# Gate products and pool channels by one level of Strassen's scheme, with reordered weight sums on GpSimd

## Chip, cores and metric

The kernel runs on one core of a Trainium2 chip. The metric is device time in microseconds (us), from runs of the whole program on that core. The engines are TensorE (PE, with its weight loads shown apart as PEld), VectorE (DVE), ScalarE (ACT), GpSimd (POOL) and SyncE (SP), which only issues transfers here.

## What is computed

One decoder layer over 512 tokens of width 1024, in fp32. The part that matters here is the head of it:

```
h = rmsnorm(x, g_mix[i])
u = h @ w_in[i]                       # 1024 -> pool 512 | q 512 | k 128 | v 128
y_a = pool_mixer(u_pool, w_pool_mix[i], pool_scale[i]) @ w_branch_a[i]
y_b = swa_attention(q, k, v, q_gain[i], k_gain[i], attn_sinks[i]) @ w_branch_b[i]
gates = jax.nn.sigmoid(h @ w_gate[i] + b_gate[i])      # 1024 -> 2048
merged = gates[..., :D] * y_a + gates[..., D:] * y_b
x = x + merged @ w_out[i]
```

`pool_mixer` takes, for each of four groups of 128 channels, the trailing mean over 2, 4, 8 or 16 tokens minus the token, and mixes the channels. The attention has 8 heads of 64 and a window of 128, and is done in four blocks of 128 tokens. Behind this stand a routed layer of 64 experts (three matrices of 1 MB each for every expert, 192 MB in all), a shared expert, and a last gated addition.

## The kernel before

The activations h are kept transposed in `actT` (128 partitions x 8 k-blocks x 512 tokens). Weights arrive in `ring`, 12 slots of 1 MB. The list `DENSE` gives the order of the weight units of the head: q0, q1, kv, pool0, pool1, gate0 to gate7, wa0, wb0, wa1, wb1, out0 to out3, shg, shu; `DENSE_SLOT` gives their slots. SyncE loads them in this order (`load_dense`, L419), each after the unit that had its slot before has been used (`released_by`, L416). Every engine runs its instructions in the order in which its block of the program is written; semaphores with names such as `pool_ps` or `gate_copied` connect them.

PE works in this order:
- the q, k, v products for four tiles of 128 tokens (L1500: 512 columns, L1506: 256 columns, 8 k-blocks each), with the transposes of q and k (L1519, L1521) behind the next tile. DVE normalises each tile in between (L982 to L998) and copies the transposes out (L974, L976), with POOL making the reciprocal roots (L621, L622);
- the pool channels: four tiles of 128 channels, 8 matmuls of 128x128 weights against 512 tokens each, into banks 0 to 3 (L1540). ACT copies them out (L758), POOL makes the windowed means (L645 to L651);
- the scores of block 0 (L1571), then 16 gate tiles (`gate_tile`, L1556), 8 matmuls of 512 columns each, alternating between PSUM banks 0 and 1. ACT copies each out with its bias (L772), and tile m waits until tile m-2 has been copied. In between stand four attention rounds: transposes of the probabilities (`probs_T`, L1588), scores of the next block, a gate tile, attention times values (`attend`, L1600), a gate tile. Four gate tiles, the pool mixing (`mix`, L1609) and two more gate tiles end it;
- the branch products wa and wb (L1641, L1643), then w_out (L1659) and what follows.

DVE does softmax: scores plus bias (L1023), maximum (L1028), small operations (L1029 to L1031), the division (L1036 to L1038), and it copies the transposed probabilities (L1048) and the attention output (L1052). ACT takes the exponentials (L764). After the last gate tile ACT makes the sigmoids of all gates (L789), and DVE multiplies and adds (L1068 to L1073).

In the expert stage PE does for each step 64 records of gate and up products (L1904) and 32 of the down product (L1933). SyncE loads an expert into its slots after PE has used what is there (L450, L469).

## Time and profile before

| | us |
|---|---|
| median of 3 runs | 1023.71 (1023.64 to 1026.5) |
| the profiled execution | 1023.04 |
| its span, first to last instruction | 1020.8 |
| PE busy | 952.3 |
| DVE busy | 297.5 |
| ACT busy | 166.2 |
| POOL busy | 167.7 |

Median and profiled execution differ by 0.67 us; 2.2 us lie around the span. Busy time of PE counts matmul records, whose ends overlap, so durations of one record are longer than the pace at which they follow each other; the chain of what ended last gives the pace. A matmul in fp32 shows as two records, each with its own weight load.

### The profile page before, as it was taken

To read this page: it belongs to the slowest core of one execution; us is meant where nothing else is said; L and a number is where in the kernel's file an instruction comes from. 1 tells how busy PE (TensorE), PEld (TensorE's weight loads), DVE (VectorE), ACT (ScalarE), POOL (GpSimd) and SP (SyncE) were. 2 spreads that over 40 slices of the span, in tenths; PEclk is the share of its full clock that TensorE was granted. 3 is DMA by queue.
4 is the path that set the end of the run, shared out by engine and by line. 5 is a ranking of instruction groups with operands and counts; after the bars stand their busy time and mean duration, and the time that the engine had idled before them with its cause. 6 is when DMAs were issued, how large, how long until landed. Compare 5 with 4: busy or idle time off the path is not lost.

```text
span 1020.8 us, 14891 instructions
## 1 busy us (share of the span) xinstructions
PE 952.3 (93%) x6015; PEld 418.7 (41%) x6015; DVE 297.5 (29%) x707; ACT 166.2 (16%) x308; POOL 167.7 (16%) x319
## 2 busy tenths in 40 slices
PE   6999999999999999999999999989969998984698
PEld 4554544444445543443333333345323333331244
DVE  3322552002224743333332111111101111110677
ACT  2002221122001121111111111111111112111021
POOL 4236000000000012222222222212121212111010
PEclk9999999999999999999999999999989999998799
DMA  9441211210191589999999999999999999996982
GB/s 336 138 146 61 83 42 42 82 67 17 40 344 42 204 316 347 417 409 412 405 412 405 411 418 401 394 416 414 397 422 421 421 421 421 418 403 256 376 298 83
DMA packets 82148, 294.90 MB, mean 289 GB/s; under 512 B 9148, under 2 KB 35680, under 8 KB 57888
## 3 DMA queue, kind: packets, MB, share of 16 engines
q1 hardware_dynamic: 67472, 255.90, 63.8%
q0 software_dynamic: 11920, 33.86, 8.5%
q10 hardware_dynamic: 2688, 4.19, 1.1%
q8 instruction: 48, 0.79, 0.3%
q14 instruction: 20, 0.16, 0.1%
HBM read 277.14 MB, written 25.17 MB: 296 GB/s over the span
## 4 chain that ended last, share of the span: by engine, by line
PE 72%; DMA 23%; DVE 2%; SPq 1%; issue 1%; ACT 0%; POOL 0%; POOLq 0%; DVEq 0%; ACTq 0%
PE ps L1904 21%; DMA ring<-in_w_exp_up 19%; PE ps L1556 11%; PE ps L1933 7%; PE ps L1659 5%; PE ps L2030 4%; PE ps L1540 3%; PE ps L1500 3%; PE ps L1643 3%; PE ps L1641 3%; PE ps L1477 2%; DMA ring<-accumulator 2%; DMA ring<-in_w_exp_down 1%; PE ps L1730 1%; PE ps L1506 1%; SPq L450 1%
## 5 line engine op out<-in xcount | busy, mean ns | idle before, releaser
L1904 PE MATMUL ps<-ring,gates 128*32 128x512 f32 x2560 | 288.5, 603 | 28.4 <-DMA ring<-in_w_exp_up 27.7
L1904 PEld LDWEIGHTS ps<-ring,gates 128*32 128x32 f32 x2560 | 88.1, 111 | 220.9 <-issue 220.0
L1933 PE MATMUL ps<-ring,poolbuf 128*32 128x512 f32 x1280 | 145.6, 595 | 3.0 <-DMA ring<-in_w_exp_down 3.0
L1318 DVE COPY poolbuf<-ps 128x256 f32<-128x256 f32 x40 | 17.0, 425 | 357.6 <-PE ps L1913 357.6
L1556 PE MATMUL ps<-actT,ring 128*128 128x512 f32 x256 | 112.3, 595 | 0.0
L661 POOL TENSOR_TENSOR tickets<-cst 128x1 f32<-128x1 f32 x77 | 14.6, 189 | 398.2 <-ACT actT L850 392.7
L1556 PEld LDWEIGHTS ps<-actT,ring 128*128 128x128 f32 x256 | 47.9, 190 | 59.6 <-issue 59.5
L1933 PEld LDWEIGHTS ps<-ring,poolbuf 128*32 128x32 f32 x1280 | 37.9, 109 | 83.4 <-issue 81.7
L850 ACT ACTIVATE actT<-ps,qT 128x1024 f32<-128x1024 f32 x40 | 44.6, 1114 | 142.2 <-PE ps L1933 142.2
L842 ACT ACTIVATE poolbuf<-ps 128x256 f32<-128x256 f32 x40 | 15.4, 385 | 281.6 <-PE ps L1904 281.6
L2030 PE MATMUL ps<-ring,actT 128*128 128x512 f32 (+1 forms) x144 | 59.8, 568 | 0.5 <-DVE actT L1434 0.5
L1477 PE MATMUL ps<-cst,rows 128*128 128x128 f32 x352 | 48.1, 283 | 9.4 <-DMA cst<-in_constants 9.1
L1659 PE MATMUL ps<-ring,gates 128*128 128x512 f32 x128 | 56.4, 594 | 0.0
L621 POOL TENSOR_SCALAR st<-st 128x1 f32<-128x1 f32 (+2 forms) x17 | 5.0, 295 | 289.2 <-ACT rows L795 227.8
L1477 PEld LDWEIGHTS ps<-cst,rows 128*128 128x128 f32 x352 | 44.5, 193 | 11.0 <-DMA cst<-in_constants 9.1
L673 POOL DMA_INDIRECT rows<-h_rows,stage x40 | 41.9, 1048 | 21.7 <-issue 19.3
L678 POOL DMA_INDIRECT accumulator<-actT,stage x40 | 40.7, 1019 | 21.8 <-issue 21.8
L2030 PEld LDWEIGHTS ps<-ring,actT 128*128 128x128 f32 x144 | 27.8, 199 | 25.4 <-issue 23.8
L1659 PEld LDWEIGHTS ps<-ring,gates 128*128 128x128 f32 x128 | 23.8, 190 | 27.3 <-issue 27.3
L1068 DVE TENSOR_TENSOR gates<-gates,ps 128x512 f32<-128x512 f32 x8 | 5.5, 687 | 91.8 <-PE ps L1643 91.8
L837 ACT ACTIVATE gates<-ps 128x512 f32<-128x512 f32 x40 | 23.9, 597 | 32.3 <-PE ps L1477 32.3
L1643 PE MATMUL ps<-qT,ring 128*128 128x512 f32 x64 | 28.8, 592 | 0.0
(242 smaller groups left out, 870.8 us busy)
## 6 DMA issues: line engine op xcount, KB each, us to landing
ring<-in_w_exp_down SPq DMA_DIRECT2D x64, 1024.0 KB, 17.4
ring<-in_w_exp_gate SPq DMA_DIRECT2D x62, 1024.0 KB
ring<-in_w_exp_up SPq DMA_DIRECT2D x62, 1024.0 KB
ring<-accumulator SPq DMA_DIRECT2D x12, 1024.0 KB, 13.8
ring<-in_w_gate SPq DMA_DIRECT2D x8, 1024.0 KB, 13.6
ring<-in_w_in SPq DMA_DIRECT2D x5, 1024.0 KB
ring<-in_w_out SPq DMA_DIRECT2D x4, 1024.0 KB
ring<-in_w_ple_gate SPq DMA_DIRECT2D x4, 1024.0 KB
```

The source lines that it names most:

```text
L673: pool.indirect_dma_start(hg[j], None, h2_dram, bass.IndirectOffsetOnAxis(ap=stage[:, 0, j, :], axis=0), bounds_check=T - 1, oob_is_err=Fa ...
L678: pool.indirect_dma_start(y_dram, bass.IndirectOffsetOnAxis(ap=stage[:, 1, j, :], axis=0), yrow[j], None, bounds_check=ACC_ROWS - 1, oob_i ...
L850: nc.scalar.activation(yrow[j], bank(6, 2), ACT.Copy, scale=slot_wr[:, r, 0:1]).then_inc(y_ready, 1)
L1477: last = nc.tensor.transpose(bank(b0 + half)[:, k * width:(k + 1) * width], v[0:width, 4 * half + k, :], ident[0:width, 0:width])
L1500: last = mm(bank(2 * (i % 2)), actT[:, k, i * P:(i + 1) * P], qv[:, k], start=(k == 0), stop=(k == KD - 1))
L1540: last = mm(bank(g), w[:, k, (g % 2) * P:(g % 2 + 1) * P], actT[:, k, :], start=(k == 0), stop=(k == KD - 1))
L1556: last = mm(bank(m % 2), w[:, k, (m % 2) * P:(m % 2 + 1) * P], actT[:, k, :], start=(k == 0), stop=(k == KD - 1))
L1643: last = mm(bank(b + 1), wb[:, k, mi * P:(mi + 1) * P], qT[:, k, :], start=(k == 0), stop=(k == 3))
L1659: last = mm(bank(half), gates[:, k, i * P:(i + 1) * P], w[:, k], start=(k == 0), stop=(k == KD - 1))
L1904: last = mm(bank(2 + k)[part, :], hgT[k][:, q, part], pair_view(EXPERT_SLOT[js[c]])[:, q], start=(q == 0), stop=(q == KD - 1))
L1933: last = mm(bank(6 + half)[part, :], eactT[r % 2][:, q, part], w[:, q, half * 512:(half + 1) * 512], start=(q == 0), stop=(q == 1))
L2030: last = mm(gate_bank(i, n0)[:, 0:width], actT[:, k, i * P:(i + 1) * P], unit_view(s, 4)[:, k % 4, n0 % 512:n0 % 512 + width], start=(k == ...
```

## The change

The product of h with a pair of weight units, 1024 x 512 by 512 tokens, is split into quarters (k-blocks 0 to 3 and 4 to 7; the first 256 channels and the second 256; tokens 0 to 255 and 256 to 511), and computed by Strassen's scheme with seven products of quarters instead of eight. A pair is pool0 with pool1, or gate p with gate p+4. Each product is a *phase*: 8 matmuls with 256 columns, 16 records, into one PSUM bank.

- DVE makes four sums of token quarters (`hsum`, 128x1024 each) once. They are written over `xrow`, so SyncE loads x again after the last phase, ahead of shg and shu, and the residual addition waits for that.
- Four sums of weight quarters are needed for each pair, one of them in place. DVE makes those of the pool pair and of gate pair 0 (`first_wsums`); they lie in `gates`, which is not yet used there. POOL makes those of pairs 1 to 3 (`weight_sums`), in ring slots whose units are done. Those of pair 1 now stand ahead of the pooled sums in POOL's order, pairs 2 and 3 behind them.
- DVE adds each finished phase into the quadrants of the result (`phase_sum`: seven phases, eight operations on 128x512). It did not touch these results before; ACT's copies L758 and L772 go. ACT takes over the copies of the transposed probabilities, and adds the gate bias in the sigmoid, pair by pair; only the last pair's sigmoids stand behind the last phase.
- PE runs 7 phases for the pool channels and 28 for the gates, two banks in turn; phase q of the gates waits until the sum of phase q-2 is done.
- The ring slots are held longer: gate3 and gate7 load after gate phase 14 is reached, wa0 and wb0 after 21, wa1, wb1 and out0 to out3 after 28. The first scores no longer wait for the pool results.

```diff
-DENSE = ["q0", "q1", "kv", "pool0", "pool1"] + [f"gate{c}" for c in range(8)] + \
+PAIRS = 4
+PHASES = 7 * PAIRS
+HALF_T = T // 2
+DENSE = ["q0", "q1", "kv", "pool0", "pool1"] + [f"gate{p + h * PAIRS}" for p in range(PAIRS) for h in range(2)] + \
...
+        hsum = [xrow[:, n, :].rearrange("p (k n) -> p k n", k=4) for n in range(4)]
+        def quarters(p):
+            names = [f"gate{p + h * PAIRS}" for h in range(2)] if p >= 0 else ["pool0", "pool1"]
+            ga, gb = (unit_view(DENSE_SLOT[DENSE_AT[u]], KD) for u in names)
+            return ga[:, 0:4, :], gb[:, 0:4, :], ga[:, 4:8, :], gb[:, 4:8, :]
+        def wsums(p):
+            if p <= 0:
+                cs = (4, 6, KD + 4) if p == 0 else (0, 2, KD)
+                flat = [gates[:, c:c + 2, :].rearrange("p a n -> p (a n)") for c in cs]
+            else:
+                s = (3, 5, 7)[p - 1]
+                s2 = (s + 1) % 8
+                flat = [ring[:, s, 0:UNIT // 2], ring[:, s, UNIT // 2:], ring[:, s2, 0:UNIT // 2]]
+            return [v.rearrange("p (k n) -> p k n", k=4) for v in flat]
...
-                           "pool0": (pool_ps, 2), "pool1": (pool_ps, NG)}
-            released_by |= {f"gate{c}": (gate_ps, 2 * c + 2) for c in range(8)}
+            released_by |= {"pool0": (gate_ps, 14), "pool1": (gate_ps, 14)}
+            released_by |= {f"gate{c}": (gate_ps, 21 if c % 2 == 0 else PHASES) for c in range(8)}
...
-            for u in range(3, N_DENSE):
+            for u in range(3, DENSE_AT["shg"]):
+                load_dense(u)
+            sp.wait_ge(gate_ps, PHASES)
+            for i in range(NT):
+                sp.dma_start(xrow[:, i, :], x_rows[i]).then_inc(x_loaded[i], 16)
+            for u in range(DENSE_AT["shg"], N_DENSE):
                 load_dense(u)
...
+            def weight_sums(p):
+                for h in range(2):
+                    u = DENSE_AT[f"gate{p + h * PAIRS}"]
+                    pool.wait_ge(slot_loaded[DENSE_SLOT[u]], 16 * (uses_before(DENSE_SLOT[u], u) + 1))
+                if p == 1:
+                    pool.wait_ge(pool_ps, 7)
+                    pool.wait_ge(wsum_ready, 8)
+                else:
+                    pool.wait_ge(gate_ps, 7 * (p - 1))
+                w11, w12, w21, w22 = quarters(p)
+                t1, t2, t4 = wsums(p)
+                for n, (dst, a, b) in enumerate(((t1, w12, w11), (t2, w22, t1), (w12, w22, w12), (t4, w21, t2))):
+                    nc.gpsimd.tensor_tensor(dst, a, b, ALU.subtract).then_inc(wsum_ready, 1)
+                    pool.wait_ge(wsum_ready, 4 * p + n + 5)
+
+            weight_sums(1)
             for g, w in enumerate(POOL_WINDOWS):
-                pool.wait_ge(upool_ready, g + 1)
+                pool.wait_ge(upool_ready, 6 + g // 2)
...
+            weight_sums(2)
+            weight_sums(3)
...
+            def phase_sum(p, n, done):
+                c11, c12, c21, c22 = (quadrant(p, t, h) for t in range(2) for h in range(2))
+                done = done.rearrange("p (f n) -> p f n", f=2)
+                if n == 0:
+                    return nc.vector.tensor_copy(c21, done)
+                dst, old = ((c12, c21), (c11, c21), (c21, c12), (c22, c21), (c21, c21), (c12, c12))[n - 1]
+                if n == 4:
+                    link(nc.vector.tensor_tensor(c12, c12, done, ALU.add))
+                return nc.vector.tensor_tensor(dst, old, done, ALU.add)
...
             softmax_scores(0)
+            gate_sum(0)
+            gate_sum(1)
+            softmax_divide(0)
+            gate_sum(2)
+            gate_sum(3)
             for n in range(NT):
-                softmax_divide(n)
-                prob_transposed(n)
                 if n + 1 < NT:
                     softmax_scores(n + 1)
+                gate_sum(4 * n + 4)
+                gate_sum(4 * n + 5)
                 attn_copy(n)
+                if n + 1 < NT:
+                    softmax_divide(n + 1)
+                gate_sum(4 * n + 6)
+                gate_sum(4 * n + 7)
+            for q in range(4 * NT + 4, PHASES):
+                gate_sum(q)
...
+            def phase(p, n, out, done):
+                w11, w12, w21, w22 = quarters(p)
+                t1, t2, t4 = wsums(p)
+                h11, h12, h21, h22 = (actT[:, 4 * c:4 * c + 4, t * HALF_T:(t + 1) * HALF_T]
+                                      for t in range(2) for c in range(2))
+                w, x = ((w11, h11), (t2, hsum[1]), (w21, h12), (w12, hsum[2]), (t1, hsum[0]), (t4, h22),
+                        (w22, hsum[3]))[n]
+                for f in range(2):
+                    for k in range(4):
+                        last = mm(out[:, f * HALF_T:(f + 1) * HALF_T], w[:, k, f * P:(f + 1) * P], x[:, k, :],
+                                  start=(k == 0), stop=(k == 3))
+                last.then_inc(done, 1)
...
             scores(0)
-            gate_tile(0)
-            gate_tile(1)
+            for q in range(4):
+                gate_phase(q)
             for n in range(NT):
                 probs_T(n)
                 if n + 1 < NT:
                     scores(n + 1)
-                gate_tile(2 + 2 * n)
+                gate_phase(4 * n + 4)
+                gate_phase(4 * n + 5)
                 attend(n)
-                gate_tile(3 + 2 * n)
-            for m in range(10, 14):
-                gate_tile(m)
+                gate_phase(4 * n + 6)
+                gate_phase(4 * n + 7)
+            for q in range(4 * NT + 4, PHASES - 2):
+                gate_phase(q)
             mix()
-            gate_tile(14)
-            gate_tile(15)
+            for q in range(PHASES - 2, PHASES):
+                gate_phase(q)
```

PE from the pool channels to the first attention round, before (L1540 pool tiles, L1519 and L1521 transposes of q and k, L1571 scores, L1556 gate tiles, L1588 transposes of probabilities):

```order
L1540 MATMUL ps<-actT,ring 128x512 x16
L1519 MATMUL ps<-cst,rows 128x128 x4
L1521 MATMUL ps<-cst,rows 128x128 x2
L1540 MATMUL ps<-actT,ring 128x512 x16
L1571 MATMUL ps<-kT,qT 128x128 x8
L1556 MATMUL ps<-actT,ring 128x512 x16
L1588 MATMUL ps<-cst,ring 128x128 x8
```

The same place in the changed kernel (L1661 phases, L1636 and L1638 transposes of q and k, L1710 scores):

```order
L1661 MATMUL ps<-actT,ring 128x256 x8
L1661 MATMUL ps<-xrow,gates 128x256 x8
L1661 MATMUL ps<-actT,ring 128x256 x8
L1661 MATMUL ps<-xrow,ring 128x256 x8
L1636 MATMUL ps<-cst,rows 128x128 x4
L1638 MATMUL ps<-cst,rows 128x128 x2
L1661 MATMUL ps<-xrow,gates 128x256 x8
L1661 MATMUL ps<-actT,gates 128x256 x8
L1661 MATMUL ps<-xrow,ring 128x256 x8
L1710 MATMUL ps<-kT,qT 128x128 x8
```

Four tiles of 8 matmuls with 512 columns have become seven phases of 8 matmuls with 256, four ahead of the last transposes and three behind.

DVE from the last tile of q and k to the maximum of block 0, before (L974, L976 copies of the transposes; L1023 scores; L1028 maximum):

```order
L998 TENSOR_TENSOR rows<-rows,st 128x512
L974 TENSOR_SCALAR qT<-ps,vecT 128x4x128
L976 TENSOR_SCALAR kT<-ps,vecT 128x2x128
L974 TENSOR_SCALAR qT<-ps,vecT 128x4x128
L976 TENSOR_SCALAR kT<-ps,vecT 128x2x128
L1023 SCALAR_TENSOR_TENSOR ring<-ps,ring 128x2x128 x4
L1028 TENSOR_REDUCE smx<-ring 128x8
```

The same place in the changed kernel (L1062, L1065, L1066 sums of phases; L1053, L1054 weight sums; L1031, L1033 copies of the transposes):

```order
L1033 TENSOR_SCALAR kT<-ps,vecT 128x2x128
L1062 COPY poolbuf<-ps 128x2x256
L1066 TENSOR_TENSOR poolbuf<-poolbuf,ps 128x2x256
L1053 TENSOR_TENSOR gates<-ring 128x1024
L1053 TENSOR_TENSOR gates<-ring,gates 128x1024
L1053 TENSOR_TENSOR ring<-ring 128x1024
L1054 TENSOR_TENSOR gates<-ring,gates 128x1024
L1066 TENSOR_TENSOR poolbuf<-poolbuf,ps 128x2x256 x2
L1031 TENSOR_SCALAR qT<-ps,vecT 128x4x128
L1033 TENSOR_SCALAR kT<-ps,vecT 128x2x128
L1065 TENSOR_TENSOR poolbuf<-poolbuf,ps 128x2x256
L1066 TENSOR_TENSOR poolbuf<-poolbuf,ps 128x2x256 x3
```

Between the two copies of transposes now stand the sums of phases 0 to 3 and the four weight sums of gate pair 0; the sums of phases 4 to 6 follow.

## Rows read from the trace of the kernel before

**Rows 1.** The page, part 1: busy us (share of the span) xinstructions.

```profile
PE 952.3 (93%) x6015; PEld 418.7 (41%) x6015; DVE 297.5 (29%) x707; ACT 166.2 (16%) x308; POOL 167.7 (16%) x319
```

**Rows 2.** Busy time by stretch of the span, the columns as the first line says.

```profile
core 0: us, PE busy (x) PEld busy (x) DVE busy (x) ACT busy (x) POOL busy (x), PEclk, DMA share, GB/s
...
59.00:88.20 29.20, 28.44 (x72) 12.70 (x71) 4.89 (x9) 2.39 (x4) 17.21 (x17) 1.00 0.46 144
88.20:226.40 138.20, 136.64 (x441) 66.06 (x442) 40.93 (x64) 28.43 (x88) 7.34 (x7) 1.00 0.18 61
226.40:281.30 54.90, 54.90 (x129) 24.30 (x128) 13.85 (x21) 10.39 (x18) 0.00 (x0) 1.00 0.11 39
...
367.50:531.50 164.00, 163.27 (x1675) 63.99 (x1675) 57.75 (x204) 27.00 (x40) 35.69 (x76) 1.00 1.00 400
531.50:932.00 400.50, 369.82 (x3020) 142.36 (x3018) 58.72 (x140) 62.06 (x97) 72.26 (x153) 0.98 1.00 409
```

**Rows 3.** Waits of SyncE's queue from 360 us: total, times, longest.

```profile
SPq L450 <- PE ps L1904: 236.1, 36, 11.9
```

**Rows 4.** The chain that ended last: start us, duration us, what.

```profile
44.04 3.45 PE ps L1506 x16
48.15 6.87 PE ps L1500 x16
55.02 3.45 PE ps L1506 x16
59.12 13.93 PE ps L1540 x32
...
88.22 1.23 PE ps L1571 x16
...
126.64 7.06 PE ps L1556 x16
...
147.26 7.06 PE ps L1556 x16
...
165.86 6.87 PE ps L1556 x16
```

**Rows 5.** PE groups by shape, until 270 us: busy, mean ns, idle before.

```profile
L1556 PE MATMUL ps<-actT,ring 128*128 128x512 f32 x256 | 112.3, 595 | 0.0
L1540 PE MATMUL ps<-actT,ring 128*128 128x512 f32 x64 | 27.9, 593 | 0.0
L1506 PE MATMUL ps<-ring,actT 128*128 128x256 f32 x64 | 14.5, 379 | 0.0
L1506 PEld LDWEIGHTS ps<-ring,actT 128*128 128x128 f32 x64 | 12.2, 190 | 3.4 <-issue 1.9
```

**Rows 6.** Waits of PE from 59 to 285 us: total, times, longest.

```profile
PE ps L1588 <- DVE ring L1048: 1.5, 4, 0.4
PE ps L1571 <- ACT poolbuf L758: 0.8, 1, 0.8
```

**Rows 7.** DVE in order of time: start, us, line, operation, idle before.

```profile
16.88 0.16 DVE L966 CAST idT<-cst 128x128 bf16<-128x128 f32 x1
25.86 0.42 DVE L982 COPY rows<-ps 128x256 f32<-128x256 f32 x1 [8.82 <-PE ps L1506]
42.85 0.47 DVE L976 TENSOR_SCALAR kT<-ps,vecT 128x256 f32<-128x256 f32 x1
64.67 0.48 DVE L976 TENSOR_SCALAR kT<-ps,vecT 128x256 f32<-128x256 f32 x1
91.72 1.14 DVE L1029 TENSOR_TENSOR smx<-smx,sink 128x8 f32<-128x8 f32 x1
92.98 0.19 DVE L1031 TENSOR_SCALAR smx<-smx 128x8 f32<-128x8 f32 x1
96.53 0.17 DVE L1036 TENSOR_TENSOR smx<-smx 128x8 f32<-128x8 f32 x1 [3.35 <-ACT smx L766]
```

**Rows 8.** POOL in order of time at the same place.

```profile
88.22 4.62 POOL L645 TENSOR_TENSOR poolbuf<-poolbuf 128x512 f32<-128x512 f32 x4 [0.41 <-ACT poolbuf L758]
```

**Rows 9.** Groups by shape, until 270 us, of DVE, ACT and POOL.

```profile
L645 POOL TENSOR_TENSOR poolbuf<-poolbuf 128x512 f32<-128x512 f32 x10 | 10.6, 1063 | 9.7 <-ACT poolbuf L758 9.2
L1048 DVE COPY ring<-ps 128x512 f32<-128x512 f32 x12 | 7.7, 686 | 13.2 <-PE ps L1588 13.0
L1038 DVE TENSOR_TENSOR ring<-ring,smx 128x2048 f32<-128x2048 f32 x3 | 6.9, 2292 | 0.1
L1028 DVE TENSOR_REDUCE smx<-ring 128x8 f32<-128x2048 f32 x3 | 6.9, 2286 | 0.1
L651 POOL TENSOR_TENSOR ring<-poolbuf 128x512 f32<-128x512 f32 x4 | 5.1, 1268 | 0.3
L1068 DVE TENSOR_TENSOR gates<-gates,ps 128x512 f32<-128x512 f32 x6 | 4.1, 687 | 82.1 <-PE ps L1643 82.1
L758 ACT ACTIVATE poolbuf<-ps 128x512 f32<-128x512 f32 x4 | 2.4, 598 | 30.0 <-PE ps L1540 30.0
L1029 DVE TENSOR_TENSOR smx<-smx,sink 128x8 f32<-128x8 f32 x4 | 1.6, 410 | 0.1
L1038 DVE TENSOR_TENSOR ring<-ring,smx 128x1024 f32<-128x1024 f32 x1 | 1.2, 1224 | 0.0
```

**Rows 10.** DMA issues until 300 us: count, KB each, median us to landing.

```profile
ring<-in_w_gate SPq DMA_DIRECT2D x8, 1024.0 KB, 13.6
```

**Rows 11.** Busy time by stretch, columns as in rows 2.

```profile
281.00:306.00 25.00, 25.00 (x59) 11.02 (x58) 5.49 (x10) 2.30 (x3) 1.59 (x2) 1.00 0.95 346
```

More of the change, by code:

```diff
@@ new lines, in gate_sigmoids @@
+            def gate_sigmoids(p):
+                act.wait_ge(gate_copied, 7 * (p + 1))
+                for m in (2 * p, 2 * p + 1):
+                    for half in range(2):
+                        c = m + half * KD
+                        nc.scalar.activation(gates[:, c, :], gates[:, c, :], ACT.Sigmoid, bias=vecT[:, c:c + 1]
+                                             ).then_inc(gates_ready, 1)
+            exps(0)
+            for n in range(NT):
+                prob_transposed(n)
+                if n + 1 < NT:
+                    exps(n + 1)
@@ L1012, in _ @@
                     qk_transposed(i - 1)
+                if i == 1:
+                    first_wsums(-1)
+            pool_sum(0)
+            pool_sum(1)
+            first_wsums(0)
+            pool_sum(2)
+            pool_sum(3)
             qk_transposed(NT - 1)
+            for n in range(4, 7):
+                pool_sum(n)
             def softmax_scores(n):
@@ new lines, in pool_phase @@
+            def pool_phase(n):
+                if n == 0:
+                    loaded("pool0")
+                    loaded("pool1")
+                    pe.wait_ge(hsum_ready, 4)
+                    pe.wait_ge(q_copied, NT)
+                    pe.wait_ge(kv_copied, NT)
+                elif n == 1:
+                    pe.wait_ge(wsum_ready, 4)
+                else:
+                    pe.wait_ge(upool_ready, n - 1)
+                phase(-1, n, bank((1 + n) % 2), pool_ps)
+            for n in range(7):
+                pool_phase(n)
+                if n == 3:
+                    qk_T(NT - 1)
@@ new lines, in gate_phase @@
+            def gate_phase(q):
+                p, n = q // 7, q % 7
+                if n == 0:
+                    loaded(f"gate{p}")
+                    loaded(f"gate{p + PAIRS}")
+                if n in (1, 3, 5):
+                    pe.wait_ge(wsum_ready, 4 * p + (6, 7, 8)[n // 2])
+                if q < 2:
+                    pe.wait_ge(upool_ready, q + 6)
+                else:
+                    pe.wait_ge(gate_copied, q - 1)
+                phase(p, n, bank((p + n) % 2), gate_ps)
```

109 lines of the change are left out of this document (54 added, 55 removed).

## Prediction, before the changed kernel ran

> **What bounds the kernel now.** I read the page's busy shares first, then stretches by stage, then the chain that ended last, then the groups of instructions by shape, and last the timelines of VectorE (DVE) and GpSimd (POOL) around the places that the change touches. The reader should see three things. First, TensorE (PE) is busy 93% of the span [rows 1]. In the stretch that the change rewrites, 59 to 226.4 us, its records cover 165.1 of 167.4 us, at a granted clock of 1.00 (the 2.4 GHz level), with DMA at 46% and then 18% [rows 2]. No transfer and no other engine ends a wait of any size there: this stretch lasts as long as PE's work. Second, the expert stage is paced by DMA (share 1.00 from 367.5 to 932 us [rows 2]), but its loads are released by PE's own steps (SyncE's load line waited 236.1 us for PE [rows 3]). So its start moves with PE, and its length, a fixed number of bytes, does not. Third, what is saved ahead of it therefore reaches the end in full, unless a new wait eats it.
>
> **Columns on PE: the main term.** A tile of pool or gate channels is 8 matmuls of 512 columns, recorded as 16 records (fp32 has two for each matmul), and takes 6.87 us in the chain [rows 4]. There are 4 + 16 of them: 64 and 256 records [rows 5]. A phase of the new scheme is 8 matmuls of 256 columns, so again 16 records. The trace of before has exactly this shape: the kv product, 16 records of 128x256, takes 3.45 us [rows 4]. There are 7 phases for the pool channels and 28 for the gates. Before: 20 x 6.87 = 137.4 us. After: 35 x 3.45 = 120.75 us. Difference **-16.65 us**. The one eighth of ideal would be 17.2; the rest goes to a small cost for each record, which 256 columns pay twice as often.
>
> Does a short matmul still hide its weight load? A load of 128x128 takes 190 ns and a record of 256 columns 216 ns (3.45/16) [rows 4, 5], so 26 ns are left, and the kv product shows no idle PE between its records (idle 0.0 in its group [rows 5]). The term stands as long as every phase streams like it. Each resumption after a transpose or attention product costs the same 0.19 us in both kernels (7.06 against 6.87 in the chain [rows 4]), and there are as many of them.
>
> **The wait of the first scores.** PE waited 0.8 us, once, ahead of the scores at 88.22 [rows 4, 6], for ScalarE's copy of the last pool tile. The new scores wait only for copies of q and kv and for the transposed q and k, all done by then. **-0.8 us**, bounds 0 and -1.0 (with the refill of the pipe).
>
> **Is VectorE in time in the pool phases?** The sums move from ScalarE to VectorE, and the order matters. Phases 0 and 1 go to two banks and run from 59.1 [rows 4] to 66.0. Phase 2 needs the sum of phase 0, which VectorE reaches after its work on the fourth tile of q and k; that ends at 64.67 + 0.48 = 65.15 [rows 7]. The sum is an operation on 512 elements of PSUM, 0.69 us [rows 9], so it ends at 65.9: just in time. I take **+0.2**, bounds 0 and +1.0. Behind the next sum stand the four weight sums of gate pair 0, each 128x1024: 1.22 us by the only row of this size [rows 9], 5.1 us with hand-over, 66.7 to 71.8. Phase 3 needs only the sum before them; phase 4 starts at 73.9 (after the last transpose, 1.0 us) and needs the sum of phase 2, ready at 72.5. Hidden, with 1.4 us to spare.
>
> The four token sums (5.1 us) fall into the 8.8 us in which VectorE waits for the first kv product, 17.0 to 25.86 [rows 7]: nothing. The pool weight sums fall behind the second tile of q and k (43.3 to 48.4 [rows 7]), so the third tile starts 0.9 us late, and its norms end near 54; PE wants them after the fourth kv product, at 58.5 [rows 4]. Nothing. If that cover were gone, each would cost up to its 5.1 us.
>
> **VectorE in the attention rounds.** A round on PE keeps its length: two tiles of 6.87 become four phases of 3.45. In before one lasts 20.6 us (the first tiles of two rounds start at 126.64 and 147.26 [rows 4]). VectorE needs in it about 5.3 for scores (four of 0.68, overlapped), maximum (2.29) and small operations, 2.7 for the division (2.29 and two small ones), 0.7 for the attention copy, and 4 or 5 sums, 3.4: 12.1 of 20.6 us [rows 9]. Capacity is there; the question is order. The division of round 0 waits for the exponentials (about 3.3 us) and stands behind the sums of phases 0 and 1: scores start at 84.3, the maximum is out 5 us later (as in before, 88.22 to 93.17 [rows 4, 7]), the exponentials by 92.7 (3.35 of idle VectorE in before [rows 7]), the second sum by 93.2, the division by 94.9. PE wants it at 99.3 (four phases from 85.5): 4.4 us to spare. In the later rounds the same count gives about 3.4 us. The tightest sum is that of phase 4 (two additions, 1.4 us): its data are there at 106, VectorE is free of the second round's scores near 107.5, so it ends at 109 and is wanted at 110.5, ahead of phase 6. ScalarE takes over the probability copies: 0.60 against 0.69 us [rows 9]; PE's 1.5 us of waits for them [rows 6] may shrink by some tenths. I take **0**, bounds -0.5 and +0.5.
>
> **POOL and its port.** The twelve weight sums of pairs 1 to 3 have no row of their size on POOL. Nearest: 1.06 us for 512 elements [rows 9], so 2.1 each (bounds 1.3 and 2.5, once and twice the 1.27 us of the pooled difference; I take twice the first row), 9 us for a pair. Pair 1 starts when the pool phases end (84.3), ends near 94 and is wanted at 125 (phases counted at 3.45, rounds at 20.6). The pooled sums follow until about 121 (wanted near 196), pair 2 until 131 (wanted at 154). Pair 3 waits for phase 13 (148.5) and for two weight units: 13.6 us of issue to landing at worst [rows 10], ends by 172, wanted at 182. All hidden.
>
> But the two engines disturb each other. At 91.72 a VectorE operation on eight elements with two SBUF inputs took 1.14 us; its three sisters average 0.17 (the group's mean is 0.41 over four [rows 9]). It ended at 92.86, as POOL's run of 4.62 us from 88.22 ended (92.84) [rows 7, 8]. I price it as one POOL operation's rest in front of a VectorE operation with two SBUF inputs. Softmax has four in a round: up to 4 x 2.1 = 8.4 us in rounds 0 and 2, where POOL makes weight sums; 4 x 1.3 = 5.2 in round 1. Less the spare times: 4.0 + 5.0 + 1.8, or 11 us at the very worst. The row shows one hit of 1 us for two candidates, so 2 us in a round, under the spare time: I take **0**, bounds 0 and +11.
>
> The Trainium skill, "SBUF — State Buffer", section "SBUF: two separate sides", has a rule against this change: the port pair shared by the two engines is an exclusive lock, held for a whole instruction, and an operation with two SBUF inputs asks for it. By that rule longer POOL instructions mean longer blocks, and the stalls would be those of the first rival below instead of none; the 1.14 us agree with it.
>
> **Transfers.** wa1, wb1 and the four units of w_out now load after the last phase, and x (2 MB) is read again: 8 MB in a stretch where 39 GB/s moved before [rows 2]. At the 346 GB/s seen from 281 us [rows 11] that is 24 us, until about 233. wa1 and wb1 come first (wanted 27 us after the phases), w_out and x are wanted after 55. The expert loads still wait for the branch product behind them. **0**; bound +2 if wa1 lands late. The sigmoids of three pairs move ahead of the branch product: 0, it never waited for them.
>
> **Sum.** Against the profiled execution, 1023.04 us (span 1020.8): -16.65 - 0.8 + 0.2 = -17.25, so 1005.8. The median of the runs is 0.67 above the profiled one: **1006.5 us**.
>
> **Rivals.** (a) *Softmax late behind port and queue.* Divisions arrive after their spare time in two or three rounds: +3 to +11, so 1009.5 to 1017.5, centre 1011. For: the 1.14 us, and POOL busy nearly throughout rounds 0 to 2. Against: spare times of 3.4 to 4.4. (b) *Slower: weight loads come out from under the short matmuls.* In 35 phases there are 560 records; if weights and columns out of other tensors streamed worse than in the kv product, with the whole 190 ns exposed, it would be +106 - 17 = 89 us, 1113. It turns into a loss from 31 ns a record (17.4/560), i.e. a record of 247 ns. Against: the kv product in this trace, at 216. (c) *Absorbed.* The expert stage starts earlier, but DMA does not, and the end stays: 1023. Against: the SyncE waits for PE. In part it could be true for the first loads, at 0.95 share [rows 11]; +1 to +3 lies in my range. (d) *More than summed:* the copy waits shrink and the first sum costs nothing: 1004 to 1005.
>
> **Chances.** Forecast within 1004 to 1009: 0.64. (a) 0.20, of which two thirds below 1012. (b) 0.04. (c) in full 0.05. (d) beyond 1004: 0.05. The rest, 0.02, is that the phases do not do what they say; but the new order lists 8 matmuls of 256 columns a phase. Range **1003.5 to 1012**: it cuts off (b), (c) and the far end of (a). A measurement tells 0.3%, about 3 us, from no change. Faster by more than that: 0.91; within: 0.05; slower: 0.04.
>
> **What would show it.** PE's matmuls of phases: 560 records of 128x256, about 120.8 us in all. Scores start at 84.3 and the branch product near 209. Waits of PE for the pool sums under 1 us, for the probabilities (divisions) none, for POOL's weight sums none. VectorE's small operations with two SBUF inputs will show 1 to 2 us here and there. The DMA-paced stage keeps its length within 2 us. I am wrong if a phase takes over 3.5 us, if PE waits over 1 us a round for the divisions, or if the expert stage gets longer.

## The result: 1023.67 to 1005.92 us

| | before | after |
|---|---|---|
| median of 4 runs each, us | 1023.67 | 1005.92 (1004.77 to 1008.41) |
| ratio of the times | | 0.9831, 95% interval 0.9815 to 0.9848 |
| profiled execution / its span, us | 1023.04 / 1020.8 | 1005.25 / 1003.4 |
| first pool product to branch product, us | 59.12 to 226.36 = 167.24 | 59.62 to 209.18 = 149.56 |
| from there to the end of the span, us | 794.44 | 794.22 |

The forecast was 1006.5 in a range of 1003.5 to 1012. I call the stretch of the fourth row *the stretch*. It got 17.7 us shorter; what lies behind it kept its length. That can be read at once in the busy time by stage, from the same view as [rows 2] (columns: stretch, its length, then busy us and count of PE, PEld, DVE, ACT and POOL, granted clock, DMA share, GB/s):

```profile
59.00:84.30 25.30, 25.30 (x124) 22.18 (x122) 14.76 (x21) 0.00 (x0) 2.16 (x2) 1.00 0.39 125
84.30:209.00 124.70, 123.33 (x634) 102.29 (x633) 61.31 (x80) 35.16 (x101) 53.69 (x34) 1.00 0.11 34
209.00:264.00 55.00, 55.00 (x130) 24.37 (x129) 14.54 (x22) 2.56 (x4) 0.00 (x0) 1.00 0.51 172
350.00:514.00 164.00, 162.79 (x1669) 63.35 (x1668) 57.90 (x204) 26.61 (x39) 35.70 (x76) 1.00 1.00 398
514.00:915.00 401.00, 368.79 (x3028) 142.79 (x3024) 58.95 (x140) 63.56 (x99) 72.26 (x153) 0.99 1.00 410
```

PE is as full as it was, at the same granted clock of 1.00. VectorE has 76 us of work in the first two rows, where it had 46 [rows 2], and POOL 56 where it had 25. The branch product now has 172 GB/s of DMA beside it, 39 before: the late weights and x, and it is still full on PE. The two last stretches are windows of nearly the same lengths as in [rows 2], shifted by 17.5 us; in them PE's busy time differs from before by 0.5 and 1.0 us, at the same DMA share of 1.00.

The chain of what ended last (start us, duration us, what), cut to the stretch:

```profile
59.62 14.01 PE ps L1661 x64
...
74.28 10.36 PE ps L1661 x48
84.64 1.19 PE ps L1710 x16
85.83 14.14 PE ps L1661 x64
...
122.13 2.50 DVE ring L1127 x4
124.65 2.30 DVE smx L1132
126.97 2.07 DVE smx L1133
129.15 2.33 DVE smx L1135
132.21 7.14 PE ps L1661 x32
...
171.02 27.82 PE ps L1661 x128
198.84 3.43 PE ps L1748 x8
202.27 6.91 PE ps L1661 x32
209.18 3.43 PE ps L1782 x8
```

L1661 is the matmul of a phase, 16 records each. Eight phases in a row take 27.82 us, 3.48 each; the forecast had 3.45 from the kv product [rows 4], and the 27.82 hold one refill of 0.2 (what PE loses when it resumes behind other matmuls, 7.06 against 6.87 us for 16 records of 512 columns in [rows 4]). In round 2 the chain leaves PE for VectorE's softmax, which nothing in the chain of before did there. PE's waits in this stretch (total, times, longest):

```profile
PE ps L1727 <- ACT ring L824: 1.2, 4, 0.3
PE ps L1661 <- DVE gates L1066: 0.2, 1, 0.2
```

They answer to [rows 6]: copies of probabilities 1.2 us instead of 1.5, the wait of the first scores gone, and 0.2 us for a sum of a phase, the only new one. The copies gave more than these waits show. One round in the chain, before and after (L1588 and L1727 are the transposes of the probabilities):

```profile
122.06 0.45 PE ps L1588 x4
122.61 0.70 DVE ring L1048
123.35 1.25 PE ps L1588 x8
```

```profile
118.63 0.45 PE ps L1727 x4
119.16 0.61 ACT ring L824
119.81 1.15 PE ps L1727 x8
```

From the first transpose to the next scores it is 2.55 us before and 2.34 after: the copy is 0.09 us shorter, the transposes behind it 0.10. Over four rounds this part of the chain goes from 9.14 to 8.39 us. So the 17.68 us come apart, with nothing left over: tiles against phases 139.11 to 122.80, -16.31; first scores -0.81; copies -0.75; the new wait for a sum +0.19.

### The profile page after: what moved, and what is told of

It is laid out like the page before. It is cut to its first block, busy times and chain, and to the rows that moved or that the text cites. A ratio compares the mean times of both kernels' runs of the same rounds, so it can differ in the third digit from the quotient of the medians.

```text
span 1003.4 us, 15465 instructions
## 1 busy us (share of the span) xinstructions
PE 934.2 (93%) x6255; PEld 464.0 (46%) x6255; DVE 337.6 (34%) x743; ACT 162.7 (16%) x304; POOL 198.7 (20%) x331
## 4 chain that ended last, share of the span: by engine, by line
PE 73%; DMA 22%; DVE 3%; SPq 1%; issue 1%; ACT 0%; POOL 0%; POOLq 0%; ACTq 0%
PE ps L2045 22%; DMA ring<-in_w_exp_up 16%; PE ps L1661 12%; PE ps L2074 9%; PE ps L1800 5%; PE ps L2171 4%; PE ps L1617 3%; PE ps L1784 3%; PE ps L1782 3%; PE ps L1594 3%; DMA ring<-accumulator 2%; DMA ring<-in_w_exp_down 1%; PE ps L1871 1%; PE ps L1623 1%; PE ps L2054 1%; DMA rows<-h_rows,stage 1%
## 5 line engine op out<-in xcount | busy, mean ns | idle before, releaser
L2074 PEld LDWEIGHTS ps<-ring,poolbuf 128*32 128x32 f32 x1280 | 37.9, 109 | 83.5 <-issue 81.8
L1661 PE MATMUL ps<-xrow,ring 128*128 128x256 f32 x256 | 57.9, 381 | 0.2 <-DVE gates L1066 0.2
L1661 PEld LDWEIGHTS ps<-xrow,ring 128*128 128x128 f32 x256 | 48.3, 190 | 8.1 <-issue 1.3
L1661 PE MATMUL ps<-actT,ring 128*128 128x256 f32 x208 | 47.5, 381 | 0.0
L1661 PEld LDWEIGHTS ps<-actT,ring 128*128 128x128 f32 x208 | 39.0, 190 | 6.8 <-issue 1.4
L689 POOL TENSOR_TENSOR ring<-ring 128x1024 f32<-128x1024 f32 x12 | 28.3, 2360 | 52.4 <-DMA ring<-in_w_gate 30.3
```

The costliest lines, as they stand in the source:

```text
L1661: last = mm(out[:, f * HALF_T:(f + 1) * HALF_T], w[:, k, f * P:(f + 1) * P], x[:, k, :], start=(k == 0), stop=(k == 3))
L2074: last = mm(bank(6 + half)[part, :], eactT[r % 2][:, q, part], w[:, q, half * 512:(half + 1) * 512], start=(q == 0), stop=(q == 1))
```

## Experiments

All of them change the changed kernel. A time is the median of the runs beside runs of the kernel before (1023.65 to 1023.9 in each series). Because the part behind the stretch adds a scatter of its own (below), the stretch is read from each profile as well. The first row has its three kernels in three series; rows two to five ran in a series without the changed kernel beside them, and their stretches are compared with 149.56.

| kernel | stretch us | median us (lowest to highest) | ratio to before, 95% |
|---|---|---|---|
| changed kernel, three times | 149.56, 149.54, 149.54 | 1005.92, 1005.5, 1007.02 | 0.9831, 0.9843, 0.9845 |
| eighth product | 166.59 | 1024.65 (1021.06 to 1027.79) | 0.9997 (0.998 to 1.0014) |
| pool phases of 128 columns | 150.38 | 1007.91 (1006.4 to 1010.96) | 0.9841 (0.981 to 0.9872) |
| pair 1's weight sums behind the pooled sums | 151.11 | 1009.38 (1007.71 to 1013.48) | 0.9868 (0.9839 to 0.9898) |
| tiny weight sums | 149.21 | not comparable | |
| first scores wait | 150.09 | 1005.01 (1003.57 to 1010.06) | 0.9828 (0.9806 to 0.9851) |
| copies on VectorE | 151.43 | 1011.18 (1007.76 to 1012.12) | 0.9879 (0.986 to 0.9897) |
| the same, pair 2 late | 151.44 | 1010.12 (1007.55 to 1011.38) | 0.9861 (0.9839 to 0.9882) |
| split transposes, pair 2 late, twice | 146.91, 146.91 | 1004.41, 1005.33 | 0.9806 (0.9786 to 0.9826), 0.9824 (0.9803 to 0.9844) |

### Is the gain the columns, and does it reach the end? (e1_eight)

```diff
-                for f in range(2):
-                    for k in range(4):
...
+                for again in range(2 if n == 6 else 1):
+                    for f in range(2):
+                        for k in range(4):
```

> The changed kernel with an eighth product: the last phase of each of the five pairs is computed twice, so PE does as many columns as before the change, 40 phases of 3.45 us. If the gain comes from the columns and what is saved ahead of the expert stage reaches the end in full, it costs 5 x 3.45 = 17.25 us: median 1023.2, branch product at 226.4, and the stretch behind it as long as in both kernels (794.3 us). If the gain came from other places (the dropped wait of the first scores, copies on ScalarE) by more than 1 us, it ends below 1022.5. If the expert stage absorbs shifts, the end moves by less than the start of the branch product.

The stretch went from 149.56 to 166.59: +17.03 for five phases, where 17.25 was expected. The ratio to before is 1 within its interval, and from the branch product to the end it took 794.0 us, as in the other two. The median was 1024.65 where I expected 1023.2; the profiled execution took 1022.71. So the columns are the gain, all but 0.65 us of it (167.24 - 166.59), and the expert stage gives neither back nor takes. The missing 0.2 has its place: in this kernel PE does not wait for a sum in round 2. The added phase of pair 0 stands ahead of it, POOL's weight sums of pair 2 are nearly over when the maximum is taken, and they hold up one operation (1.02 us at L1133) instead of two (4.4 us, see below).

### Do weight loads have only 26 ns to spare? (e2_narrow)

```diff
+                cut = 2 if p < 0 else 1
+                c = HALF_T // cut
                 for f in range(2):
-                    for k in range(4):
-                        last = mm(out[:, f * HALF_T:(f + 1) * HALF_T], w[:, k, f * P:(f + 1) * P], x[:, k, :],
-                                  start=(k == 0), stop=(k == 3))
+                    for h in range(cut):
+                        for k in range(4):
+                            last = mm(out[:, f * HALF_T + h * c:f * HALF_T + (h + 1) * c], w[:, k, f * P:(f + 1) * P],
+                                      x[:, k, h * c:(h + 1) * c], start=(k == 0), stop=(k == 3))
```

> The seven pool phases alone with matmuls of 128 columns: the same columns in twice as many matmuls, 32 records a phase, each with its own weight load. If a weight load occupies its 190 ns, so that 256 columns had 26 ns to spare (the prediction's reading), a phase takes 32 x 0.19 = 6.1 us, the pool phases 18.4 us longer: about 1024.3. If the 190 ns are mostly latency and the columns alone set the pace, 32 x 0.109 = 3.5 us a phase, +0.3 us: about 1006.2.

PE in order of time, two of the seven phases:

```profile
62.83 3.74 PE L1664 MATMUL ps<-xrow,gates 128*128 128x128 f32 x32
66.41 3.74 PE L1664 MATMUL ps<-actT,ring 128*128 128x128 f32 x32
```

From one start to the next it is 3.58 us for 32 records: 112 ns each, though a weight load shows 192 ns in these phases. So that is how long a load lasts, not how often one can start, and the 26 ns were no margin in that sense: against a pace of 112 ns, a record of 216 has over 100 to spare. The price of the first reading (18.4 us) is void, and with it the mechanism of rival (b). Its 31 ns a record is only the cost at which the change would break even, and stands as that. The measured cost is 0.12 us a phase, 0.84 for seven (stretch +0.82); I had expected 0.3, and a median of 1006.2 where 1007.91 came. From 216 to 429 ns (3.45 and 6.87 us for 16 records [rows 4]) is 213 ns for 256 columns, 107 for 128; so a record costs its columns and, by this estimate, some 2 to 3 ns at 256 columns, about 5 at 128.

### What do POOL's weight sums cost? (e4_tiny_sums)

```diff
-                    nc.gpsimd.tensor_tensor(dst, a, b, ALU.subtract).then_inc(wsum_ready, 1)
+                    nc.gpsimd.tensor_tensor(dst[:, :, 0:1], a[:, :, 0:1], b[:, :, 0:1], ALU.subtract).then_inc(wsum_ready, 1)
```

> POOL's twelve weight sums work on one column of each k-block only (4 elements instead of 1024), so the gates of pairs 1 to 3 are not those of the reference; all else is as in the changed kernel. Theory of the port: the one-input operation that took 2.33 us in rounds 0 and 2 falls to about 0.2 in round 2, the maximum of round 2 is out about 4 us earlier (near 127.5), PE's 0.18 us wait for a sum at 132.2 is gone. The time hardly moves, 1005.7, since nearly all of it lay in spare time. Rival: the weight sums cost PE something that the waits do not show; then it is 1 us or more faster.

The whole took 3074.86 us and says nothing: the kernel's further rounds over all experts run (1024 records of 128x512 at L2131, a line that does nothing in the changed kernel), I take it because other gates route the tokens unevenly. The stretch is untouched by that. VectorE in round 2, first the changed kernel, then this one (start us, us, line, operation):

```profile
126.97 2.06 DVE L1133 TENSOR_TENSOR smx<-smx,sink 128x8 f32<-128x8 f32 x1
129.06 0.17 DVE L1134 TENSOR_TENSOR smx<-sink,smx 128x8 f32<-128x8 f32 x1
129.15 2.33 DVE L1135 TENSOR_SCALAR smx<-smx 128x8 f32<-128x8 f32 x1
131.39 1.47 DVE L1066 TENSOR_TENSOR gates<-gates,ps 128x512 f32<-128x512 f32 x2
```

```profile
126.26 0.17 DVE L1133 TENSOR_TENSOR smx<-smx,sink 128x8 f32<-128x8 f32 x1
126.47 0.17 DVE L1134 TENSOR_TENSOR smx<-sink,smx 128x8 f32<-128x8 f32 x1
126.55 0.16 DVE L1135 TENSOR_SCALAR smx<-smx 128x8 f32<-128x8 f32 x1
126.62 0.68 DVE L1066 TENSOR_TENSOR gates<-gates,ps 128x512 f32<-128x512 f32 x1
```

And POOL in the changed kernel at that place:

```profile
121.78 9.67 POOL L689 TENSOR_TENSOR ring<-ring 128x1024 f32<-128x1024 f32 x4
```

Two operations on eight elements took 4.4 us instead of 0.3; in the changed kernel POOL's four instructions follow each other every 2.4 us, and each of the two ended as one of them did (129.03 and 131.47 against 129.01 and 131.44). With the sums made tiny the delays are gone, and so is PE's wait for the sum at 132.2. The stretch is 0.35 us shorter: all that the weight sums cost PE, 0.18 of it that wait, and 0.11 to 0.13 a pause ahead of phase 2, for the sum of phase 0, too short for the list of waits (the first four gate phases take 14.12 to 14.14 us in the changed kernel, 14.01 here). The theory held, with one thing that the prediction did not have: L1135 has a single SBUF input, and was held up just like L1133.

### Is the second part of the change, pair 1 ahead of the pooled sums, worth anything? (e3_pool_order)

```diff
-            weight_sums(1)
             for g, w in enumerate(POOL_WINDOWS):
...
+            weight_sums(1)
             weight_sums(2)
             weight_sums(3)
```

> The weight sums of pair 1 behind the pooled sums on POOL, as they would stand without the second part of the change. Theory: POOL's order has spare time either way. Pooled sums from 82 to about 108, pair 1 until 118, wanted at 126; pair 2 until 128, wanted at 156: same time as the changed kernel, 1005.9 within 0.5. Rival: softmax of round 1 now meets 2.1 us weight sums, and PE waits for the division or for pair 1's sums: +1 us and more, and a wait of PE shows it.

The rival won. PE and VectorE in round 1 (in brackets: idle before, and what ended it):

```profile
112.72 3.72 PE L1661 MATMUL ps<-xrow,ring 128*128 128x256 f32 x16 [1.83 <-DVE gates L1066]
```

```profile
106.75 2.17 DVE L1133 TENSOR_TENSOR smx<-smx,sink 128x8 f32<-128x8 f32 x1
108.95 0.17 DVE L1134 TENSOR_TENSOR smx<-sink,smx 128x8 f32<-128x8 f32 x1
109.04 2.33 DVE L1135 TENSOR_SCALAR smx<-smx 128x8 f32<-128x8 f32 x1
```

Pair 1's sums run from 106.55 to 116.2 in this order, right across the maximum of round 1. VectorE loses 4.2 us on two operations, the sum of phase 4 (two additions) comes late, and PE waits 1.83 us. The stretch is 1.55 us longer. It is not the weight sums that came late, which is what one would guard against, but a sum of VectorE that has nothing to do with POOL's results. In the order of the change the same two hits fall on rounds 0 and 2, where a single addition stands behind the maximum and not the two of a fifth phase; in round 2 that one is late by 0.18 us. The 1.55 us are the 1.83 less the 0.11 and 0.18 of the changed kernel, which are gone here.

### The wait of the first scores (e5_scores_wait)

```diff
                 else:
+                    pe.wait_ge(upool_ready, 7)
                     pe.wait_ge(q_copied, NT)
```

> The first scores wait for all seven pool sums again. The sum of the last pool phase ended 0.8 us after the scores began in the changed kernel (84.68 + 0.69 against 84.57), so by the prediction's second term PE stands for 0.8 to 1.0 us there: stretch 150.4 to 150.6. Rival: the wait is hidden, because the gate phase behind it would have been held up anyway: stretch 149.6.

```profile
85.06 1.24 PE L1711 MATMUL ps<-kT,qT 64*128 64x128 f32 x16 [0.83 <-issue]
```

The view names no engine for this wait; the last pool sum ended at 84.97, 0.09 us ahead of the scores. PE stood for 0.83 us, but the stretch grew by only 0.55 (150.09, where 150.4 to 150.6 was expected): with PE later by that much, the small waits for sums in rounds 0 and 2 (0.11 and 0.18 us) were gone. The term of -0.8 was right where it stands, and worth 0.55 net. In the medians it cannot be seen.

### Copies of the probabilities on VectorE (e6_dve_copies, e7_copies_late)

ScalarE's loop over the rounds loses `prob_transposed(n)`, and VectorE's gets it:

```diff
-                    nc.scalar.activation(probT[:, b, o:], bank(6 + b % 2)[:, o:], ACT.Copy).then_inc(probT_ready, 1)
...
+                    nc.vector.tensor_copy(probT[:, b, o:], bank(6 + b % 2)[:, o:]).then_inc(probT_ready, 1)
...
             for n in range(NT):
+                prob_transposed(n)
                 if n + 1 < NT:
                     softmax_scores(n + 1)
                 gate_sum(4 * n + 4)
```

> The copies of the transposed probabilities go back from ScalarE to VectorE, ahead of the scores' additions. Theory: each of the four waits of PE grows by the 0.09 us by which VectorE's copy is slower, and the additions of the next block start 0.4 to 0.7 us later, which falls on the sum that PE waits for in round 2 (0.18 us now): stretch 150.2 to 150.8, 0.6 to 1.2 us more. Rival: VectorE has no room for them in the rounds in which POOL holds it up, and PE waits for divisions or sums by 2 us or more: 152 and up.

Stretch 151.43, +1.9, above what either number of the theory said and just under the rival's. PE waited 2.9 us for these copies:

```profile
100.64 0.77 PE L1727 MATMUL ps<-cst,ring 128*128 128x128 f32 x4 [0.68 <-DVE ring L1152]
120.04 1.25 PE L1727 MATMUL ps<-cst,ring 128*128 128x128 f32 x8 [0.51 <-DVE ring L1152]
141.56 1.25 PE L1727 MATMUL ps<-cst,ring 128*128 128x128 f32 x8 [1.23 <-DVE ring L1152]
162.37 1.25 PE L1727 MATMUL ps<-cst,ring 128*128 128x128 f32 x8 [0.51 <-DVE ring L1152]
```

For the 1.23 us in round 2 I suspected POOL, and moved its weight sums of pair 2 behind phase 12:

```diff
-                    pool.wait_ge(gate_ps, 7 * (p - 1))
+                    pool.wait_ge(gate_ps, 12 if p == 2 else 14)
```

> Copies of the probabilities on VectorE as in the experiment before, but POOL's weight sums of pair 2 only after phase 12. There PE's longest wait for a copy, 1.2 us in round 2, was taken to come from VectorE being held up by POOL. If so it falls to the 0.5 us of the other rounds, and the stretch goes from 151.4 to about 150.7. If it came from the order of VectorE's own work alone, both stay. The median of the experiment before was 5.5 us above the changed kernel though its stretch was only 1.9 us longer; if that rest was chance in the DMA-paced part, this kernel's median lies within 2.5 us of the changed kernel's.

Nothing moved: 1.2 us again, stretch 151.44. So it is VectorE's own order. The trace of the kernel before this one could have told me: there POOL's sums of pair 2 end at 131.0, long before the copies at 140.8, and here they run from 139.7 to 149.3, right across them, and the four copies last 0.68 or 0.69 us each in both. The copies stand behind the sums of the two phases ahead of them, and in round 2 one of these is the fifth phase of a pair, with two additions, from 139.50 to 140.91. The changed kernel's copy starts 0.70 us after the first transpose; here that would be 140.0, and it starts at 140.83. ScalarE has nothing to do from 136 to 143. Moving the copies to it was a needed part of the change, worth 1.9 us of PE against leaving them on VectorE. The forecast never priced that alternative: it compared only the durations of the copies (0.60 against 0.69 [rows 9]) in the kernel before. The median, 1010.12, lies 3.1 us above that of the changed kernel beside it, not within the 2.5 that would have made the excess of the other version chance; more on this below.

### A shorter stretch (v1_split_late, v1_again)

```diff
             for n in range(NT):
-                probs_T(n)
+                probs_T(n, 0)
                 if n + 1 < NT:
                     scores(n + 1)
-                gate_phase(4 * n + 4)
+                    probs_T(n, 1)
+                    gate_phase(4 * n + 4)
+                else:
+                    gate_phase(4 * n + 4)
+                    probs_T(n, 1)
                 gate_phase(4 * n + 5)
```

with POOL's pair 2 behind phase 12 as above; `probs_T(n, half)` does two of its four blocks.

> Two moves in the attention rounds of the changed kernel. The scores of the next block stand between the first two and the last two probability transposes (in the last round a gate phase does), so that PE has work while ScalarE copies; and POOL starts the weight sums of pair 2 only after phase 12, when the maximum of round 2 is long out. If the four waits of 0.3 us for copies, each with a refill, and the 0.18 us wait for a sum are all that is left on PE, the stretch gets 1.5 to 2 us shorter, 147.6 to 148.1, and the median about 1004.3. Rival: the scores' additions on VectorE, which wait for the last transpose, start 0.4 us later while PE is 0.4 us ahead, and PE then waits for a sum instead: stretch within 0.5 of 149.6.

```profile
118.80 2.10 PE L1710 MATMUL ps<-kT,qT 64*128 64x256 f32 x16
120.83 1.09 PE L1727 MATMUL ps<-cst,ring 128*128 128x128 f32 x8
121.75 3.62 PE L1661 MATMUL ps<-xrow,ring 128*128 128x256 f32 x16
```

No wait of PE for another engine is left in the stretch, and it is 2.63 us shorter, more than the 1.5 to 2 that I expected. PE has work while ScalarE copies, and three refills are gone as well (6.91 instead of 7.10 us for the two phases behind the transposes). Two moves were made at once, and no run separates them. The late weight sums of pair 2 leave the maximum of round 2 alone (0.17 us each for L1133 and L1135 at 126.80 and 127.08); with the 4 us of the changed kernel added there, the sum of phase 8 would have ended near 131.8, an estimate, and was wanted at 130.8. So the split alone would have kept a wait in round 2.

> The changed kernel unaltered, as the measure for the other kernels beside it: 1005.9 us; the stretch from the first pool product to the branch product 149.6 us, as in its first profile, within 0.2.

> The kernel with the split transposes and the late weight sums of pair 2 once more, to tell it from the changed kernel by more executions. Its stretch was 146.9 against 149.5 us, so if what is saved ahead of the expert stage reaches the end, its median lies 2.6 us below that of the changed kernel beside it, about 1003; if the DMA-paced part absorbs it, the two medians agree within 1 us.

> The changed kernel unaltered, as the measure beside it: median 1005.5 to 1006, stretch 149.5.

The measures beside it were 1005.5 (expected 1005.9) and 1007.02 (expected 1005.5 to 1006, so 1 us off), both with the stretch that I expected, 149.54. The version's medians are 1.1 and 1.7 us below them; from the stretch it should be 2.6. The second was to be either 2.6 us below or within 1 us; it is neither. It is the fastest kernel here, but its ratios (0.9806 and 0.9824) and those of the changed kernel (0.9843 and 0.9845) have overlapping intervals, so the runs alone do not separate the two. The profile does, up to the branch product.

### What the DMA-paced part adds

Behind the stretch, the kernels need 793.4 to 798.9 us, with the same work. From the first expert step on, their steps keep the same distances within 0.5 us for 156 us (in one profile of the changed kernel within 0.9). Then, where PE begins to wait for DMA, they spread: the second half of the gate and up products of the last of the 40 steps starts 546.8 to 548.5 us after the first step in three profiles of the changed kernel, 549.8 in the one before, 549.3 and 550.2 in the two of the shorter version, 548.1 and 549.5 with copies on VectorE. That is as much as the small experiments are worth, and it is why I read them from the stretch.

A larger part lies behind the DMA-paced steps. From the start of the last step to the end of the span (columns as in the busy time by stage above; rows: before, the changed kernel's first and third profile, the shorter version, and the copies on VectorE with pair 2 late):

```profile
912.80:1020.80 108.00, 78.73 (x312) 36.49 (x304) 58.18 (x72) 16.01 (x30) 11.31 (x24) 0.90 0.71 261
894.40:1003.40 109.00, 79.46 (x312) 36.72 (x304) 58.19 (x72) 16.00 (x30) 11.31 (x24) 0.91 0.70 254
892.90:1004.10 111.20, 81.76 (x312) 37.79 (x304) 58.18 (x72) 16.00 (x30) 9.17 (x24) 0.88 0.68 250
892.50:1002.60 110.10, 80.68 (x312) 37.02 (x304) 58.19 (x72) 16.00 (x30) 11.27 (x24) 0.89 0.70 254
896.90:1009.50 112.60, 83.14 (x312) 37.98 (x304) 58.19 (x72) 15.99 (x30) 9.16 (x24) 0.86 0.67 245
```

PE does the same 312 records, but is busy for 78.7 and 79.5 us with them at a granted clock of 0.90 and 0.91, and for up to 83.1 at 0.86, a mean over time at the 2.4 and the 1.2 GHz level; VectorE's busy time does not change. The last row is 3.6 us longer than the second, of the 4.6 us by which all that lies behind the stretch is longer. The changed kernel's own third profile is 2.2 us longer than its first, at 0.88, so the same program shows both. Its 15 runs say the same of the whole: the seven with a mean clock of 0.983 or more took 1004.1 to 1006.59 us, the eight at 0.981 or less 1005.46 to 1013.17. So a good part of the scatter goes with the granted clock behind the steps and not with what an experiment changed. Whether the rest belongs to the kernels or to chance is open: the two versions with copies on VectorE had medians 3 to 5.7 us above the changed kernel beside them for 1.9 us of stretch, and the shorter version kept only about half of its gain. No run tells which, nor what lowers the clock in one run and not in the next.

## Why the prediction held, and where it was off

| step of the prediction | forecast | measured |
|---|---|---|
| columns, 35 phases for 20 tiles | -16.65 | -16.31; 17.03 come back when five phases are added (forecast 17.25) |
| wait of the first scores | -0.8 | -0.81; 0.55 come back when it is put back |
| sum of the first pool phase | +0.2 | 0.0 |
| softmax, sums, port | 0 (0 to +11) | +0.19 for the sum of phase 8; 0.35 is all that goes without POOL's sums |
| probability copies | 0 (-0.5 to +0.5) | -0.75 |
| the stretch | -17.25 | -17.68 |
| behind it | 0 | -0.2 |
| profiled execution | 1005.8 | 1005.25 |

**Columns.** Right, from the one row of the same shape. To find a shape already in the trace and take its pace from the chain, not the mean of its records (379 ns in [rows 5], against 216), was the step that carried the forecast. The term was 0.3 us too large; 0.11 of it is the short wait for the sum of phase 0 and 0.1 the pace (3.453 for 3.45, 35 times).

**Copies.** This term lies outside its bounds. PE's waits shrank by the forecast tenths, but the transposes behind each wait became shorter too. That the sum came within 0.5 us of the stretch is in part luck: 0.75 us more from the copies, against 0.3 less from the columns.

**Weight loads.** The size of the margin was wrong, as e2_narrow shows; the conclusion stood, since the kv product did.

**The first pool phases.** Forecast just in time, and it was: VectorE's copy of phase 0 ran from 65.60 to 66.28, and phase 2 followed phase 1 without a gap (63.10, 66.55, 70.00 are the starts). The +0.2 was not needed there; that as much went into another sum, that of phase 8, is chance. The four weight sums of pair 0 took 67.36 to 72.4 (I had 66.7 to 71.8).

**Attention rounds.** The spare times of 3.4 to 4.4 us were taken without POOL. Here is what was left of them:

| round | division ready | wanted | POOL took |
|---|---|---|---|
| 0 | 97.2 | 99.8 | 3.6 |
| 1 | 116.25 | 118.5 | 1.5 |
| 2 | 138.4 | 139.2 | 4.1 |

I had allowed 2 us a round. Rounds 0 and 2 cost twice that, and in round 2 less than 1 us was left. The forecast of no wait for a division held. What gave way first was something else: the sum of phase 8, which stands behind the maximum in VectorE's queue, 0.18 us late. I had named the sum of phase 4 as the tightest; it ended at 110.01 and was wanted at 111.45 in the changed kernel, and became the bound only in e3_pool_order. The mis-sized term here is the port: I priced one hit a round on operations with two SBUF inputs, from one row.

The rule that I had set beside this row, the Trainium skill, "SBUF — State Buffer", section "SBUF: two separate sides", names two kinds of VectorE operation that ask for the shared pair: those with two SBUF inputs, and those in a 2-port mode. I used only the first. The 2.33 us of L1135, a one-input operation between SBUF tensors, agree with the second; that it ran in such a mode no row here shows. The whole-instruction block agrees too: 2.33 us against 2.36 for a weight sum.

**POOL.** A weight sum took 2.36 us (28.3 us for twelve); forecast 2.1, bounds 1.3 to 2.5. Pair 3 came nearest to its date: POOL waited until 161.7 for gate3 and gate7, 11 us after phase 13 ended, and was done at 171.4, wanted at 181.

**Rivals.** (a), divisions late, happened in no kernel here. Its port mechanism is real, and one order of POOL away it cost PE 1.83 us, but by way of a sum that stands behind the maximum. (b) is ruled out in size by the phases themselves, at 216 ns a record, and in mechanism by e2_narrow. (c), absorption: ruled out by e1_eight for 17 us; for 2.6 us it is open. (d), more than summed: both of its conditions came true, the cheaper copies and the free first sum, and the stretch is 0.4 us shorter than summed; the profiled execution, 1005.25, lies 0.25 us above its upper end.

## To carry to other kernels

Where PE is full, as here, one level of Strassen's scheme gave its eighth (17.2 us of 137.4) less 2 to 3 ns a record. It could, because the additions fit into idle time of other engines and their order left each in-order queue ready when PE asked. Price such a change from a matmul of the new shape in the trace you have. Check long elementwise instructions on POOL against the short ones on VectorE that stand in a latency chain: what costs is not POOL's throughput but where its instructions lie in time, and an operation on eight elements can take 2.3 us. When waits of a few tenths remain, put other matmuls between a transpose and the use of its copy, and judge such changes by the stretch that they touch, because the end of this kernel moved by up to 9 us between runs of the same program, and its stretch by 0.02 us between profiles.

## What I had not expected of the hardware

- A weight load of 128x128 in fp32 shows 190 to 192 ns, yet records follow each other every 112 ns at 128 columns and every 216 at 256. Here a load's duration was no bound on the pace.
- A VectorE operation on eight elements with a single SBUF input was blocked for a whole POOL instruction, 2.33 us, and a division of 2.29 us became 2.91 beside POOL. The blocking goes both ways: four POOL additions of 512 elements took 6.54 us instead of 4.62 when the division ran, all of it in one that lasted 2.97 us instead of 1.04. Not every VectorE operation was held up: beside the weight sums of pair 2 in e7_copies_late, copies from PSUM (0.68), the scores' additions with one input in PSUM (0.68) and the maximum over 2048 elements (2.29) kept their durations.
- The changed kernel's last 312 records took 79.5 us of busy time in one profile and 81.8 in another, at mean granted clocks of 0.91 and 0.88: 2.2 us of the whole time, with the same program.
